# Attention projections: six products of a token block alternate between two weight halves, 128 bytes further apart

## The chip, the cores and the metric

The kernel runs on one core of a Trainium2 chip, in one launch. The metric is device time in microseconds of a whole run; the median of several runs counts. TensorE (PE in the profile, with its weight loads as PEld) multiplies, VectorE (DVE) and ScalarE (ACT) prepare operands and read results, GpSimd (POOL) helps, and SyncE (SP) issues nearly all loads.

## The reference, cut to what matters

Three transformer blocks run one after the other on 256 tokens of width 1024, all in float32. Each block does the following, with other attention rules in each:

```python
h = rms_norm(x, gain)
qkv = h @ w_qkv          # 1024 -> 9216 columns (first block), 3072 (second), 1536 + side columns (third)
x = x + attention(qkv) @ w_o
u = rms_norm(x, gain2) @ w_up
x = x + (silu(conv(u)[gate]) * conv(u)[val]) @ w_down
```

What concerns this change is `h @ w_qkv`.

## The kernel before, in words

**Split operands.** Every large product is made in three products of a rounded type: a float32 operand is split into a high part (rounded) and a low part (the rest), and hi·hi + hi·lo + lo·hi is summed in PSUM. The normalised tokens are held in `xg[:, k, x, :]`: `k` is one of 8 blocks of the 1024 inputs (`KT` = 8), `x` = 0 is the high part and `x` = 1 the low one, and the last index is the token. DVE makes the low part (L524) and counts `x_lo` up by one for every `k`.

**The weight stream.** All weights are read from memory in chunks of up to 1024 columns of 128 rows, in the order of use, into a ring of six buffers (`RING`). `load` in SyncE's program issues one chunk when `w_lo_done` says that the buffer six chunks ago has been split. ACT copies the chunk into `w_hi` (L418) and DVE writes `w_raw - w_hi` into `w_lo` (L426); TensorE waits for `w_lo_done`. The first three chunks are loaded and split in two halves (`half_split_hi`, `half_split_lo`, `load_half`).

**A projection chunk.** A "unit" is 384 result columns (`UNIT`; 392 for the first of the third block, `UNIT_F`) for all 256 tokens. It takes four chunks (`UCH`), and each chunk holds the weights of two blocks `k = 2q` and `k = 2q + 1`: two halves of 384 columns, one behind the other (`QCHUNK` = 768 columns). In `unit_chunk_pe` TensorE makes 12 products of a chunk: for each half `kk` and each block `t` of 128 tokens it makes three. The stationary operand is a 128×128 piece of `xg` and the moving operand is the weight half, 384 columns:

```python
nc.tensor.matmul(out, hi, wh, ...)   # L717
nc.tensor.matmul(out, hi, wl, ...)   # L718
nc.tensor.matmul(out, lo, wh, ...)   # L719
```

The two token blocks go to two banks of PSUM. A few chunks at the start of the first and second block (`EARLY`: the first four, and one) have an order of their own in `early_chunk_pe` (L643), and go on as parts of their operands become ready.

**Where the operands lie.** Buffers are laid one behind the other in the order in which they are named: six `w_raw` of 4096 bytes per partition, six `w_hi` of 4096, six `w_lo` of 4352 (a chunk and 64 spare columns), `x_all` of 8256, and `xg` of 16384. Within its buffer `w_lo` begins 16 or 32 columns in (`lo_at`: 64 or 128 bytes; 64 in all projections of attention). One column of a partition is 4 bytes, and a half is 1536 bytes.

**Other large products.** In the feed-forward stages the tokens move and the weights are stationary: the up projection makes a product of 512 columns (L458) and one of 256 (L460) for each `k`, the down projection three of 256 (L1897 to L1899). Six chunks ahead of the third block use three of 256 as well (L444 to L446).

**Order.** Each engine runs a program written out by hand, and PE's puts other work of attention (transposes, scores, sums with the values) between projection chunks. Nothing reorders it but the semaphores.

Of the kernel before, what the change touches and what calls it, by code (L numbers as in the profile page):

```python
# [49 lines left out]
LO_UP, LO_DOWN = 16, 32  # L50
CHUNK = KT * P
UNIT = 3 * P
QCHUNK = 2 * UNIT
UNIT_F = UNIT + HEADS_C
QCHUNK_F = 2 * UNIT_F
UCH = KT // 2


# [141 lines left out]
def build(nc, x_d, xa_d, stream_d, par_d, con_d, taps_d, out_d):  # L200
# [227 lines left out]


    def half_split_hi(eng, c, kk):  # L430
        part = slice(kk * UNIT, (kk + 1) * UNIT)
        eng.wait_ge(half_in[c] if kk == 0 else w_loaded[c], 16)
        nc.scalar.activation(w_hi[c][:, part], w_raw[c][:, part], ACT.Copy).then_inc(half_hi if kk == 0 else w_hi_done, 1)

    def half_split_lo(eng, c, kk):
        part = slice(kk * UNIT, (kk + 1) * UNIT)
        eng.wait_ge(half_hi if kk == 0 else w_hi_done, c + 1)
        nc.vector.tensor_tensor(w_lo(c)[:, part], w_raw[c][:, part], w_hi[c][:, part].bitcast(F32),
                                ALU.subtract).then_inc(half_lo if kk == 0 else w_lo_done, 1)
# [194 lines left out]
    def early_chunk_pe(eng, st, n):  # L634

        q, u = divmod(n, 2) if st == 0 else (n, 0)
        c = QKV_C0[st] + n
        s, k0 = c % RING, KT * 2 * st

        def term(x, part, kk, start=False, ends=False):  # L640
            k = 2 * q + kk
            for t in range(2):
                last = nc.tensor.matmul(bank(unit_bank(st, u, t), 0, UNIT), xg[:, k, x, t * P:(t + 1) * P],  # L643
                                        part[:, kk * UNIT:(kk + 1) * UNIT], start=start, stop=ends)
                if ends and t == 0:
                    last.then_inc(att[st].unit, 1)
            return last

        if st == 0 and n < HALVES:
            for kk in range(2):  # L650
                eng.wait_ge(half_hi if kk == 0 else w_hi_done, c + 1)
                eng.wait_ge(x_hi, 2 * q + kk + 1)
                term(0, w_hi[s], kk, start=(q == 0 and kk == 0))
                if u == 0:
                    eng.wait_ge(half_lo if kk == 0 else w_lo_done, c + 1)
                    term(0, w_lo(c), kk)
                eng.wait_ge(x_lo, 2 * q + kk + 1)
                last = term(1, w_hi[s], kk)
                if u == 1:
                    eng.wait_ge(half_lo if kk == 0 else w_lo_done, c + 1)  # L660
                    last = term(0, w_lo(c), kk)
        else:
            eng.wait_ge(w_hi_done, c + 1)
            eng.wait_ge(x_hi, k0 + 2 * q + 2)
            for kk in range(2):
                term(0, w_hi[s], kk)
            eng.wait_ge(x_lo, k0 + 2 * q + 2)
            for kk in range(2):
                term(1, w_hi[s], kk)
            eng.wait_ge(w_lo_done, c + 1)  # L670
            for kk in range(2):
                last = term(0, w_lo(c), kk, ends=(2 * q + kk == KT - 1))
        last.then_inc(tiles, 1)
# [9 lines left out]
    def unit_chunk_pe(eng, st, n):  # L683

        if (st, n) in EARLY:
            early_chunk_pe(eng, st, n)
            return
        a = att[st]
        u, q = divmod(n, UCH)
        if st == 0 and n < 2 * UCH:  # L690
            q, u = divmod(n, 2)
        c = QKV_C0[st] + n
        s = c % RING
        eng.wait_ge(w_lo_done, c + 1)
        if q == 0:
            if st == 0 and u > 2:
                if (u - 2) % 3 < 2:
                    eng.wait_ge(a.nm, 2 * (2 * ((u - 2) // 3) + (u - 2) % 3 + 1))
                    if (u - 2) % 3 == 0 and u - 2 >= joint_unit(0):
                        eng.wait_ge(a.olo, (u - 2) // 3 - 1)  # L700
                else:
                    v_wait(eng, 0, (u - 2) // 3)
            if st > 0 and u >= 2:
                eng.wait_ge(a.nm, 2 * (u - 1))
                eng.wait_ge(a.ve, 2 * (u - 1))
            if st == 2 and u < 2:
                eng.wait_ge(pre_out, (3, N_PRE)[u])
        width = UNIT_F if st == 2 and u == 0 else UNIT
        for kk in range(2):
            k = 2 * q + kk  # L710
            wh, wl = w_hi[s][:, kk * width:(kk + 1) * width], w_lo(c)[:, kk * width:(kk + 1) * width]
            if st < 2 and u == 0:
                eng.wait_ge(x_lo, KT * 2 * st + k + 1)
            for t in range(2):
                out = bank(unit_bank(st, u, t), 0, width)
                hi, lo = xg[:, k, 0, t * P:(t + 1) * P], xg[:, k, 1, t * P:(t + 1) * P]
                nc.tensor.matmul(out, hi, wh, start=(k == 0), stop=False)  # L717
                nc.tensor.matmul(out, hi, wl, start=False, stop=False)  # L718
                last = nc.tensor.matmul(out, lo, wh, start=False, stop=(k == KT - 1))  # L719
                if k == KT - 1 and t == 0:  # L720
                    last.then_inc(a.unit, 1)
        last.then_inc(tiles, 1)

    def unit_wait(eng, st, u, t):
# [1542 lines left out]
    with nc.Block() as block:  # L2267

        @block.sync
        def _(sp):  # L2270
            def load(c):
                s, w = c % RING, chunk_cols(c)
                sp.dma_start(w_raw[s][:, 0:w], stream_d[c, :, 0:w]).then_inc(w_loaded[s], 16)


            def load_half(c, kk):
                part = slice(kk * UNIT, (kk + 1) * UNIT)
                sp.dma_start(w_raw[c][:, part], stream_d[c, :, part]).then_inc(half_in[c] if kk == 0 else w_loaded[c], 16)

            def load_x(m, n, landed):  # L2280
                a, b = GAINS + m * TOK if m else 0, GAINS + (m + n) * TOK
                sp.dma_start(x_all[:, X0 - GAINS + a:X0 - GAINS + b], xa_d[:, a:b]).then_inc(landed, 16)

            load_x(0, 1, x_first)
            load_x(1, 1, x_in[0])
            for kk in range(2):
                load_half(1, kk)
            load_x(2, 2, x_in[1])
            for kk in range(2):
                load_half(2, kk)  # L2290
            load(3)
            load_x(4, 2, x_in[2])
            load(4)
            load(5)
            load_x(6, 2, x_in[3])
            sp.dma_start(con[:, 0:CON_MASKA], con_d[:, 0:CON_MASKA]).then_inc(con_in, 16)
            sp.dma_start(par[:, 0:PAR_FFN], par_d[:, 0:PAR_FFN]).then_inc(row_in, 16)
            for c in range(RING, N_CHUNKS):
                sp.wait_ge(w_lo_done, c - RING + 1)
                load(c)  # L2300
                if c == RING + 10:
                    sp.dma_start(con[:, CON_MASKA:], con_d[:, CON_MASKA:N_CON]).then_inc(rest_in, 16)
                if c == A_OUT:
                    sp.wait_ge(rest_in, 16)
                    sp.dma_start(par[:, PAR_FFN:], par_d[:, PAR_FFN:]).then_inc(rest_in, 16)
                if c == A_FFN:
                    sp.dma_start(mask_b, con_d[:, CON_MASK2:CON_MASK2 + 3 * P]).then_inc(taps_in, 16)
                if c == B_FFN + 2 * RING:
                    sp.wait_ge(att[1].mx, PAIRS_AB)
                    sp.wait_ge(taps_in, 16)  # L2310
                    sp.dma_start(taps[:], taps_d[:, :]).then_inc(taps_in, 16)
                if c == RING + 16:
                    sp.wait_ge(x_lo, KT)
                    sp.wait_ge(x_sq, KT)
                    for q in range(UCH):
                        sp.dma_start(xT[:, 2 * q:2 * q + 2], x_d[2 * q:2 * q + 2].rearrange("k p t -> p k t")).then_inc(x_in[q], 16)
            for m in range(0, KT, 2):
                sp.wait_ge(x_new, 5 * KT + m + 1)
                sp.dma_start(out_d[m], xT[:, m, :]).then_inc(stored, 16)
            sp.wait_ge(stored, 16 * KT)  # L2320
# [15 lines left out]
        @block.scalar  # L2336
        def _(act):
            for kk, landed in ((0, half_in[0]), (1, w_loaded[0])):
                part = slice(kk * UNIT, (kk + 1) * UNIT)
                act.dma_start(w_raw[0][:, part], stream_d[0, :, part]).then_inc(landed, 16)  # L2340
            nc.scalar.preload_act_table_set("natural_log_exp_and_others")
            half_split_hi(act, 0, 0)
# [89 lines left out]
def weight_stream(w):  # L2432
# [7 lines left out]
    def unit(cols):  # L2440

        width = sum(m.shape[1] for m in cols)
        for q in range(UCH):
            c = np.zeros((P, CHUNK), np.float32)
            for kk in range(2):
                k = 2 * q + kk
                c[:, kk * width:(kk + 1) * width] = np.concatenate([m[k * P:(k + 1) * P] for m in cols], axis=1)
            chunks.append(c)

    def outs(m, order):  # L2450
# [136 lines left out]
```

## Time and profile before

| what | value |
|---|---|
| median of 3 runs | 1027.61 us (1026.99 to 1027.81) |
| the profiled execution, its own time | 1026.79 us |
| its span, first to last instruction | 1024.9 us |
| PE busy | 1019.7 us (99%) |
| DVE, ACT, POOL busy | 879.9, 684.8, 350.3 us |
| granted TensorE clock | full, in all 40 slices |

The profiled execution lies 0.8 us under the median and has 1.9 us around its span. A product's recorded duration (about 340 ns for 384 columns) overlaps its neighbours, so the time that it costs is the distance from its start to the start of the next one. Starts are shown to 10 ns; over a run of many products the mean distance is known far better.

### The profile page before, as it was taken

To read this page: it belongs to the slowest core of one execution; us is meant where nothing else is said; L and a number is where in the kernel's file an instruction comes from. 1 tells how busy PE (TensorE), PEld (TensorE's weight loads), DVE (VectorE), ACT (ScalarE), POOL (GpSimd) and SP (SyncE) were. 2 spreads that over 40 slices of the span, in tenths; PEclk is the share of its full clock that TensorE was granted. 3 is DMA by queue.
4 is the path that set the end of the run, shared out by engine and by line. 5 is a ranking of instruction groups with operands and counts; after the bars stand their busy time and mean duration, and the time that the engine had idled before them with its cause. 6 is when DMAs were issued, how large, how long until landed. Compare 5 with 4: busy or idle time off the path is not lost.

```text
span 1024.9 us, 22177 instructions
## 1 busy us (share of the span) xinstructions
PE 1019.7 (99%) x8000; PEld 958.8 (94%) x8000; DVE 879.9 (86%) x1532; ACT 684.8 (67%) x1263; POOL 350.3 (34%) x370
## 2 busy tenths in 40 slices
PE   9999999999999999999999999999999999999998
PEld 8999999999999999999999899999998998999998
DVE  7987778787799998887887999988897879999886
ACT  7776676766766656577786766656696767565663
POOL 5312222121356533332111556333350025654332
PEclk9999999999999999999999999999999999999999
DMA  9754465554476656536454666666534536665651
GB/s 317 259 151 152 139 185 157 168 177 164 156 227 206 213 194 185 181 94 203 140 184 145 225 207 219 193 200 186 160 120 135 166 122 209 218 210 192 197 163 42
DMA packets 57896, 183.59 MB, mean 179 GB/s; under 512 B 6368, under 2 KB 9824, under 8 KB 57568
## 3 DMA queue, kind: packets, MB, share of 16 engines
q1 hardware_dynamic: 56960, 181.72, 55.7%
q8 instruction: 45, 0.74, 0.3%
q10 hardware_dynamic: 864, 0.92, 0.3%
q14 instruction: 27, 0.22, 0.1%
HBM read 181.56 MB, written 1.05 MB: 178 GB/s over the span
## 4 chain that ended last, share of the span: by engine, by line
PE 97%; DVE 2%; DMA 0%; ACT 0%; issue 0%; DVEq 0%
PE ps L458 22%; PE ps L460 11%; PE ps L717 10%; PE ps L719 10%; PE ps L718 9%; PE ps L1897 6%; PE ps L1898 6%; PE ps L1899 6%; PE ps L1363 2%; PE ps L1365 2%; PE ps L1364 2%; PE ps L643 1%; PE ps L915 1%; PE ps L810 1%; DVE w_lo L426 1%; PE ps L953 1%
## 5 line engine op out<-in xcount | busy, mean ns | idle before, releaser
L426 DVE TENSOR_TENSOR w_lo<-w_raw,w_hi 128x1024 fp32r<-128x1024 f32 (+2 forms) x369 | 440.4, 1211 | 31.4 <-ACT w_hi L418 30.8
L418 ACT ACTIVATE w_hi<-w_raw 128x1024 fp32r<-128x1024 f32 (+2 forms) x369 | 353.5, 972 | 116.4 <-PE ps L460 99.1
L458 PE MATMUL ps<-xg,w_hi 128*128 128x512 f32 x1056 | 363.1, 390 | 0.0
L460 PE MATMUL ps<-xg,w_lo 128*128 128x256 f32 x1056 | 291.5, 276 | 0.0
L458 PEld LDWEIGHTS ps<-xg,w_hi 128*128 128x128 f32 x1056 | 198.2, 188 | 40.1 <-DVE w_lo L426 0.8
L2022 POOL TENSOR_TENSOR prob_t<-prob_t,qkT 128x256 f32<-128x256 f32 x63 | 111.7, 1773 | 255.4 <-ACT prob_t L1943 255.4
L460 PEld LDWEIGHTS ps<-xg,w_lo 128*128 128x128 f32 x1056 | 198.2, 188 | 0.0
L717 PE MATMUL ps<-w_hi,xg 128*128 128x384 f32 (+1 forms) x556 | 192.3, 346 | 0.0
L719 PE MATMUL ps<-w_hi,xg 128*128 128x384 f32 (+1 forms) x556 | 187.3, 337 | 0.0
L718 PE MATMUL ps<-w_lo,xg 128*128 128x384 f32 (+1 forms) x556 | 185.7, 334 | 0.0
L1897 PE MATMUL ps<-g_hi,w_hi 128*128 128x256 f32 x528 | 146.1, 277 | 0.1
L1898 PE MATMUL ps<-g_lo,w_hi 128*128 128x256 f32 x528 | 145.8, 276 | 0.0
L1899 PE MATMUL ps<-g_hi,w_lo 128*128 128x256 f32 x528 | 145.8, 276 | 0.0
L2016 POOL TENSOR_TENSOR qkT<-prob,rms_r 128x256 f32<-128x256 f32 x132 | 123.7, 958 | 17.0 <-DVE prob L1957 12.0
L1990 DVE SCALAR_TENSOR_TENSOR qkT<-qkT,par 128x255 f32<-128x255 f32 (+1 forms) x264 | 112.3, 476 | 7.3 <-ACT qkT L1936 7.3
L1936 ACT ACTIVATE qkT<-qkT,par 128x256 f32<-128x256 f32 x132 | 78.0, 599 | 48.6 <-POOL qkT L2016 47.3
L717 PEld LDWEIGHTS ps<-w_hi,xg 128*128 128x128 f32 x556 | 104.2, 187 | 2.5 <-issue 1.5
L719 PEld LDWEIGHTS ps<-w_hi,xg 128*128 128x128 f32 x556 | 104.4, 188 | 0.0
L718 PEld LDWEIGHTS ps<-w_lo,xg 128*128 128x128 f32 x556 | 104.3, 188 | 0.1
L1897 PEld LDWEIGHTS ps<-g_hi,w_hi 128*128 128x128 f32 x528 | 99.1, 188 | 2.9 <-issue 0.4
L1898 PEld LDWEIGHTS ps<-g_lo,w_hi 128*128 128x128 f32 x528 | 99.1, 188 | 0.0
L1899 PEld LDWEIGHTS ps<-g_hi,w_lo 128*128 128x128 f32 x528 | 99.1, 188 | 0.0
(197 smaller groups left out, 1377.1 us busy)
## 6 DMA issues: line engine op xcount, KB each, us to landing
w_raw<-w_stream SPq DMA_DIRECT2D x228, 512.0 KB, 3.8
w_raw<-w_stream SPq DMA_DIRECT2D x137, 384.0 KB, 3.6
w_raw<-w_stream SPq DMA_DIRECT2D x4, 392.0 KB, 3.1
con<-consts SPq DMA_DIRECT2D x1, 1024.0 KB, 6.8
x_all<-x_t SPq DMA_DIRECT2D x4, 256.0 KB, 4.9
conv_taps<-taps SPq DMA_DIRECT2D x1, 1024.0 KB, 6.1
w_raw<-w_stream SPq DMA_DIRECT2D x4, 192.0 KB, 4.4
x_all<-x_a SPq DMA_DIRECT2D x3, 256.0 KB, 5.9
```

The source lines that it names most:

```text
L418: nc.scalar.activation(w_hi[s][:, 0:w], w_raw[s][:, 0:w], ACT.Copy).then_inc(w_hi_done, 1)
L426: nc.vector.tensor_tensor(w_lo(c)[:, 0:w], w_raw[s][:, 0:w], w_hi[s][:, 0:w].bitcast(F32), ALU.subtract).then_inc(w_lo_done, 1)
L458: nc.tensor.matmul(bank(b, 0, 2 * TOK), w_hi[s][:, k * P:(k + 1) * P], xg[:, k, :, :].rearrange("p h t -> p (h t)"), start=(k == 0), stop= ...
L460: last = nc.tensor.matmul(bank(b), w_lo(c)[:, k * P:(k + 1) * P], xg_hi[:, k, :], start=False, stop=(k == KT - 1), skip_group_check=True)
L717: nc.tensor.matmul(out, hi, wh, start=(k == 0), stop=False)
L718: nc.tensor.matmul(out, hi, wl, start=False, stop=False)
L719: last = nc.tensor.matmul(out, lo, wh, start=False, stop=(k == KT - 1))
L1897: nc.tensor.matmul(acc(m), wh, g_hi[b][:], start=first, stop=False, skip_group_check=True)
L1898: nc.tensor.matmul(acc(m), wh, g_lo[b][:], start=False, stop=False, skip_group_check=True)
L1899: last = nc.tensor.matmul(acc(m), wl, g_hi[b][:], start=False, stop=True, skip_group_check=True)
L1990: nc.vector.scalar_tensor_tensor(cv_s[b][s][:, k:TOK], up_s[b][s][:, 0:TOK - k], par_col(f, t, per, i, 4 * s + 2 - k), cv_s[b][s][:, k:TOK ...
L2016: nc.gpsimd.tensor_tensor(up_s[t % 2][s], up_sum[s], rms_r[:], ALU.mult).then_inc(F.up, 1)
```

## The change

The second half of a projection chunk no longer begins where the first ends but 32 columns (128 bytes) later: its offset `SECOND` is 416 columns instead of 384, for `w_raw`, `w_hi`, `w_lo` and in memory. A chunk so grows from 768 to 800 columns (from 784 to 808 for the unit with 392), all of which are loaded and split. And `unit_chunk_pe` makes its 12 products in another order: the token block is the outer loop, then the term (hi·wh, lo·wh, hi·wl), and the half is the inner loop. The count of products and their operands are the same. The wait for the tokens' low part, where there is one, asks for both blocks `k` before the first product of the chunk.

```diff
+SECOND = UNIT + 32
-QCHUNK = 2 * UNIT
+QCHUNK = SECOND + UNIT
-QCHUNK_F = 2 * UNIT_F
+QCHUNK_F = SECOND + UNIT_F
...
     def half_split_hi(eng, c, kk):
-        part = slice(kk * UNIT, (kk + 1) * UNIT)
+        part = slice(kk * SECOND, kk * SECOND + UNIT)
...
-                                        part[:, kk * UNIT:(kk + 1) * UNIT], start=start, stop=ends)
+                                        part[:, kk * SECOND:kk * SECOND + UNIT], start=start, stop=ends)
...
-        for kk in range(2):
-            k = 2 * q + kk
-            wh, wl = w_hi[s][:, kk * width:(kk + 1) * width], w_lo(c)[:, kk * width:(kk + 1) * width]
-            if st < 2 and u == 0:
-                eng.wait_ge(x_lo, KT * 2 * st + k + 1)
-            for t in range(2):
-                out = bank(unit_bank(st, u, t), 0, width)
-                hi, lo = xg[:, k, 0, t * P:(t + 1) * P], xg[:, k, 1, t * P:(t + 1) * P]
-                nc.tensor.matmul(out, hi, wh, start=(k == 0), stop=False)
-                nc.tensor.matmul(out, hi, wl, start=False, stop=False)
-                last = nc.tensor.matmul(out, lo, wh, start=False, stop=(k == KT - 1))
-                if k == KT - 1 and t == 0:
-                    last.then_inc(a.unit, 1)
+        w_part = [[part[:, kk * SECOND:kk * SECOND + width] for kk in range(2)] for part in (w_hi[s], w_lo(c))]
+        if st < 2 and u == 0:
+            eng.wait_ge(x_lo, KT * 2 * st + 2 * q + 2)
+        for t in range(2):
+            out = bank(unit_bank(st, u, t), 0, width)
+            for x, low in ((0, 0), (1, 0), (0, 1)):
+                for kk in range(2):
+                    k = 2 * q + kk
+                    last = nc.tensor.matmul(out, xg[:, k, x, t * P:(t + 1) * P], w_part[low][kk], start=(k == 0 and x + low == 0),
+                                            stop=(k == KT - 1 and low == 1))
+            if q == UCH - 1 and t == 0:
+                last.then_inc(a.unit, 1)
         last.then_inc(tiles, 1)
...
-                part = slice(kk * UNIT, (kk + 1) * UNIT)
+                part = slice(kk * SECOND, kk * SECOND + UNIT)
                 sp.dma_start(w_raw[c][:, part], stream_d[c, :, part]).then_inc(half_in[c] if kk == 0 else w_loaded[c], 16)
...
-                c[:, kk * width:(kk + 1) * width] = np.concatenate([m[k * P:(k + 1) * P] for m in cols], axis=1)
+                c[:, kk * SECOND:kk * SECOND + width] = np.concatenate([m[k * P:(k + 1) * P] for m in cols], axis=1)
```

## Rows read from the trace of the kernel before

**Rows 1.** The page: the chain that ended last, share of the span by engine.

```profile
PE 97%; DVE 2%; DMA 0%; ACT 0%; issue 0%; DVEq 0%
```

**Rows 2.** Waits of PE: who waited for what, us in total, times, longest.

```profile
PE ps L2327 <- DVE zero L2379: 1.1, 1, 1.1
PE ps L643 <- ACT w_hi L433: 0.4, 1, 0.4
PE ps L1363 <- DVE mix_lo L992: 0.3, 1, 0.3
```

**Rows 3.** Groups by shape on PE: busy us, mean ns of one, idle before.

```profile
L717 PE MATMUL ps<-w_hi,xg 128*128 128x384 f32 x540 | 186.7, 346 | 0.0
```

**Rows 4.** PE's timeline in a projection of the first block: start us, us, what.

```profile
23.27 0.33 PE L717 MATMUL ps<-w_hi,xg 128*128 128x384 f32 x1
23.44 0.33 PE L718 MATMUL ps<-w_lo,xg 128*128 128x384 f32 x1
23.61 0.34 PE L719 MATMUL ps<-w_hi,xg 128*128 128x384 f32 x1
23.79 0.33 PE L717 MATMUL ps<-w_hi,xg 128*128 128x384 f32 x1
...
30.55 0.33 PE L717 MATMUL ps<-w_hi,xg 128*128 128x384 f32 x1
```

**Rows 5.** PE's timeline in an up projection of a feed-forward stage.

```profile
300.05 0.39 PE L458 MATMUL ps<-xg,w_hi 128*128 128x512 f32 x1
...
302.77 0.39 PE L458 MATMUL ps<-xg,w_hi 128*128 128x512 f32 x1
```

**Rows 6.** PE's timeline in the six chunks ahead of the third block.

```profile
743.30 0.28 PE L444 MATMUL ps<-xg,w_hi 128*128 128x256 f32 x1
...
751.50 0.28 PE L444 MATMUL ps<-xg,w_hi 128*128 128x256 f32 x1
...
755.14 0.28 PE L444 MATMUL ps<-xg,w_hi 128*128 128x256 f32 x1
...
760.58 0.28 PE L444 MATMUL ps<-xg,w_hi 128*128 128x256 f32 x1
```

**Rows 7.** PE's timeline at other projection chunks of the second and third block.

```profile
457.94 1.56 PE L643 MATMUL ps<-w_hi,xg 128*128 128x384 f32 x8
459.34 0.86 PE L643 MATMUL ps<-w_lo,xg 128*128 128x384 f32 x4
...
474.60 0.34 PE L718 MATMUL ps<-w_lo,xg 128*128 128x384 f32 x1
...
478.44 0.34 PE L719 MATMUL ps<-w_hi,xg 128*128 128x384 f32 x1
...
760.92 0.34 PE L717 MATMUL ps<-w_hi,xg 128*128 128x392 f32 x1
...
764.86 0.34 PE L718 MATMUL ps<-w_lo,xg 128*128 128x392 f32 x1
```

**Rows 8.** DVE's and PE's timeline where the second block's projections begin.

```profile
451.59 0.48 DVE L524 SCALAR_TENSOR_TENSOR xg<-x_all,par,xg 128x256 fp32r<-128x256 f32 x1
...
451.69 0.34 PE L717 MATMUL ps<-w_hi,xg 128*128 128x384 f32 x1
...
453.26 0.63 DVE L524 SCALAR_TENSOR_TENSOR xg<-x_all,par,xg 128x256 fp32r<-128x256 f32 x1
```

**Rows 9.** Groups by shape on DVE: the splits of whole and of projection chunks.

```profile
L426 DVE TENSOR_TENSOR w_lo<-w_raw,w_hi 128x1024 fp32r<-128x1024 f32 x228 | 300.4, 1333 | 29.5 <-ACT w_hi L418 29.1
...
L426 DVE TENSOR_TENSOR w_lo<-w_raw,w_hi 128x768 fp32r<-128x768 f32 x137 | 136.0, 1014 | 1.8 <-ACT w_hi L418 1.6
```

**Rows 10.** Busy time of PE, PEld, DVE, ACT, POOL in the first block's projections; clock, DMA.

```profile
13.50:245.00 231.50, 231.39 (x2173) 227.32 (x2171) 183.54 (x351) 162.09 (x334) 62.62 (x81) 1.00 0.59 186
```

**Rows 11.** DVE's and PE's timeline at the fifth chunk, near the start.

```profile
12.30 1.93 DVE L426 TENSOR_TENSOR w_lo<-w_raw,w_hi 128x768 fp32r<-128x768 f32 x2
...
13.53 0.33 PE L717 MATMUL ps<-w_hi,xg 128*128 128x384 f32 x1
```

More of the change, by code:

```diff
@@ L2276, in load_half @@
             def load_half(c, kk):
-                part = slice(kk * UNIT, (kk + 1) * UNIT)
+                part = slice(kk * SECOND, kk * SECOND + UNIT)
                 sp.dma_start(w_raw[c][:, part], stream_d[c, :, part]).then_inc(half_in[c] if kk == 0 else w_loaded[c], 16)
@@ L2338, in _ @@
             for kk, landed in ((0, half_in[0]), (1, w_loaded[0])):
-                part = slice(kk * UNIT, (kk + 1) * UNIT)
+                part = slice(kk * SECOND, kk * SECOND + UNIT)
                 act.dma_start(w_raw[0][:, part], stream_d[0, :, part]).then_inc(landed, 16)
```

## The prediction

> **What bounds the kernel now.** I read the chain that ended last first: 97% of it is PE [rows 1]. Then PE's waits: three, 1.8 us together, none in a projection chunk [rows 2]. So PE has no hole to close, and a change inside the projections counts by what it does to the distance between one product's start and the next one's, almost one for one.
>
> The groups by shape give the count: 540 products of 384 columns on each of three lines [rows 3]. With the 48 of 392 columns (four chunks of 12) the changed function makes 1668, which is the 144 chunks of the three blocks, less five early ones, times 12. The mean duration in that group, 346 ns, is no price, since neighbours overlap. The timeline is. In a projection three products take 0.17, 0.17 and 0.18 us, and from 23.27 to 30.55 lie 42 distances: 7.28 / 42 = 173.3 ns each [rows 4].
>
> Is 173.3 ns what 384 columns must take? In an up projection 768 columns (512 + 256) take 2.72 us / 8 = 340.0 ns [rows 5], that is 0.4427 ns a column, and the same 113.3 ns for 256 columns stand in the settled part of the chunks ahead of the third block (5.44 us / 48) [rows 6]. By that rate 384 columns take 170.0 ns. A projection product so pays 3.3 ns more than the best rate of this trace. That is the whole room: 3.3 x 1620 = 5.4 us, and for the 392 columns (179.1 ns from 3.94 us / 22 [rows 7], against 173.5 by rate) 5.6 x 48 = 0.3 us. Together 5.7 us.
>
> What the 3.3 ns are, the trace does not say, but it gives three hints. First, the extra is not spread evenly: the longest of the three distances, 0.18 us, follows L719, after which the next product (L717) again reads `w_hi`, while after L717 and L718 the reading goes over to the other buffer [rows 4]. By the sizes in the code `w_hi` halves all begin at the same place modulo 256 bytes, and `w_lo` 64 bytes off it. Second, where each half is read twice in a row (the early chunk, L643), the distance is 1.40 us / 8 = 175.0 ns [rows 7]. Reading on at the same place modulo 256 so goes with the longer distances. Third, the same code with the same offsets modulo 256 runs at 8.20 us / 69 = 118.8 ns in three chunks and at 113.3 in the next three [rows 6]: the state in which the stream of products happens to run matters too, not the addresses alone.
>
> **The change part by part.** *The second half's place and the order.* The new order reads, in each token block, `w_hi` at 0, 128, 0, 128 and `w_lo` at 64, 192 (modulo 256, counted from `w_hi`). No product is followed by one that begins at the same place. The kind of step that costs 0.18 us is gone and all six are steps of 64 or 128. The trace has no step of 128, so I bound it: not under 170.0 (the best rate), and not over 175.4 (the 392-column products, whose second half is off by a distance that is no multiple of 256: 179.1 x 384 / 392 [rows 7]). For the value I take the two steps that do move, now: with the third between 175 and 180 ns, the other two share 520 less that, 170 to 172.5 each; the middle is 171.2 ns. That gains 2.1 x 1620 = 3.4 us. The 392-column products, if they come to the same rate (174.8), gain 4.3 x 48 = 0.2 us. Sum: 3.6 us; bounds: gain 5.7, loss 2.1 x 1668 = 3.5.
>
> On what moves an interval at all, the Trainium skill speaks against this change: "TensorE: Matmul & The Clock Gate", Step-by-step, says that TensorE reads the moving operand and the weights through two independent ports, so that loading the next weights takes nothing from the running product. By that rule no place of one operand against the other would cost anything and the sum would be zero gain. The 118.8 against 113.3 ns of one code [rows 6] shows that something beyond the column count does set the distance, though not which.
>
> *The wait for the low parts.* It exists only in the first unit of the first two blocks. In the second block, PE's first product stands at 451.69, right behind the stage before, and needs the low part of `k` = 0 alone; the low part of `k` = 1 ends at 451.59 + 0.48 = 452.07 [rows 8]. Before, the second half came 6 x 0.173 = 1.04 us later, which hid it. Now the chunk waits from 451.69 to about 452.1: 0.4 us, and the whole of PE's program is queued behind. The next chunk starts at 452.1 + 2.08 = 454.2; the low part of `k` = 3 is done at 453.26 + 0.63 = 453.89 [rows 8], so it does not wait. In the first block DVE makes the low parts ahead of the splits for which the same chunks wait anyway: nothing. Loss: 0.4 us.
>
> *32 more columns a chunk.* DVE's split costs (1333 - 1014) / 256 = 1.25 ns a column [rows 9], so 40 ns more for each of 137 whole chunks, 5.5 us in all; ACT and the loads grow by 4% as well. What hides it: in the first block's projections DVE is busy 183.5 of 231.5 us, ACT 162.1, DMA 59% [rows 10]; 93 splits x 40 ns take DVE to 187.2. The nearest point is the fifth chunk: two splits run from 12.30 to 14.23, so its own ends near 13.2 and PE starts at 13.53 [rows 11]. That lead of 0.3 us loses two splits' growth, 0.08 us. I count nothing; without any cover it would be the 5.5 us.
>
> *The earlier end of block 0.* In a unit's last chunk the first bank is complete after 6 products instead of 9, 0.52 us sooner. DVE and ACT may start reading sooner, but PE waits for none of them [rows 2]: nothing.
>
> *Sum.* -3.6 + 0.4 = -3.2 us: the profiled execution would go from 1026.79 to 1023.6. The median of the runs lies 0.8 us higher, so 1027.6 - 3.2 = 1024.4 us.
>
> **The rivals.** *No change.* The distance may depend on the moving read's start only modulo 128 (then 0 and 128 are one place), or on the state of the stream. For it: halves and ring buffers differ by multiples of 256 in every projection, so the trace never shows a step of 128. Against it: nothing direct. Then only the wait is left: 1027.6 + 0.4 = 1028.0 us. The skill's rule of two ports ends here too.
>
> *Slower: the streams no longer settle.* The settled run of 173.3 ns is one pattern of three products. Other patterns of the same lines are longer: 3.84 us / 22 = 174.5 ns in a run of the second block, 175.0 ns where each half comes twice in a row, 175.4 by the 392-column products [rows 7]; the unsettled 256-column products pay 5.5 ns over their rate [rows 6]. Six products with six different starts may have no settled pattern. At 175.0: 1.7 x 1668 + 0.4 = +3.2, 1030.8 us; at 175.4, 1031.5. It is slower by over the bound once the mean is above 174.3 ns. Against it: steps that move the start are the shorter ones in [rows 4].
>
> *DVE becomes the bound.* If the splits' growth came through in the chunks near the start or where attention's chain is tight, up to 5.5 us less the gain: 1027.6 - 3.2 + 5.5 = 1029.9. DVE's 21% of idle time [rows 10] speaks against it.
>
> **How the numbers follow.** About 0.2% (2.1 us) is what a measurement of this kernel can tell from no change. Faster by more needs a mean under 171.8 ns. Chances: the forecast's mechanism with a mean between 170 and 171.8, 0.47 (its own range 1022.0 to 1025.5); little or nothing, 0.28 (1025.5 to 1029.6); streams that do not settle, 0.22 (1029.7 to 1032, and above); DVE, 0.03. The range of 8 in 10 takes the first two and the nearer half of the third: 1022 to 1031.
>
> **What would show it.** In the timeline of a first-block projection six distances should sum to some 1.03 us instead of 1.04, with none of 0.18; a mean of 173 or more proves the forecast's main step wrong, whatever the total. The second block's first chunk should show a wait of PE of 0.4 us behind L524. DVE's split of 800 columns should take about 1.05 us with no wait of PE for it; such waits would make the covered term wrong. Another way to be wrong is a gain in the products that comes back as PE's waits for attention's own chain, which now has no wait to show its margin.

## The result and the profile after

The change makes the kernel slower: 1031.18 us (median of 6 runs, 1030.91 to 1031.7) against 1027.11 (1026.88 to 1027.81). The ratio is 1.0037, 95% interval 1.0028 to 1.0047, so +0.37%. The forecast was 1024.4 us with a range of 1022 to 1031; the median lies 0.2 us above the range, and on the other side of the kernel before. The profiled execution took 1031.7 us with a span of 1029.9.

The granted clock is full in all slices, as before. The chain that ended last, in the profile after, is as much PE's as before [rows 1], and PE's waits have one more line, the last:

```profile
PE 96%; DVE 2%; ACT 0%; DMA 0%; issue 0%; DVEq 0%; ACTq 0%
```

```profile
PE ps L2327 <- DVE zero L2379: 1.1, 1, 1.1
PE ps L1363 <- DVE mix_lo L992: 0.3, 1, 0.3
PE ps L644 <- ACT w_hi L434: 0.3, 1, 0.3
PE ps L718 <- DVE xg L525: 0.3, 1, 0.3
```

That wait is where the second block begins. In the timelines of DVE and PE there (the product's line is now L718, the low part's L525) the low part of `k` = 1 ends at 454.96 + 0.48 = 455.44, and the first product starts behind it, where it started at once before [rows 8]. In the last fence the first line is of the profile before, the others are of that after:

```profile
454.96 0.48 DVE L525 SCALAR_TENSOR_TENSOR xg<-x_all,par,xg 128x256 fp32r<-128x256 f32 x1
```

```profile
451.57 0.28 PE L1899 MATMUL ps<-g_hi,w_lo 128*128 128x256 f32 x1
...
455.01 0.28 PE L1899 MATMUL ps<-g_hi,w_lo 128*128 128x256 f32 x1
455.58 0.94 PE L718 MATMUL ps<-w_hi,xg 128*128 128x384 f32 x4 [0.29 <-DVE xg L525]
```

PE is idle for 0.29 us, but its next start comes later by more: from the last product of the stage before to the first of the projection it is 0.57 us, where before it was 451.69 - 451.57 = 0.12. So the wait costs 0.45 us.

The rest is in the products. In PE's timeline of a projection neighbours with one key are now one row; between the two `w_lo` rows lie 24 products:

```profile
71.94 0.51 PE L718 MATMUL ps<-w_lo,xg 128*128 128x384 f32 x2
72.29 0.86 PE L718 MATMUL ps<-w_hi,xg 128*128 128x384 f32 x4
72.98 0.52 PE L718 MATMUL ps<-w_lo,xg 128*128 128x384 f32 x2
...
76.17 0.51 PE L718 MATMUL ps<-w_lo,xg 128*128 128x384 f32 x2
```

4.23 us / 24 = 176.3 ns, where [rows 4] gave 173.3. For a mean over the kernel I take all 1487 distances between two neighbouring 384-column products that stand inside an unbroken run, without the first distance of a run and without the early chunks: 173.49 ns before, 175.74 after. So 2.25 ns x 1620 products of 384 columns = 3.6 us, and with the wait 4.1: about the 4.07 us between the medians. The 48 products of 392 columns did not change (183.7 and 183.4 ns in the mean of all their distances). (The two profiled spans differ by 4.9. In the profiled execution after, the early chunks also ended 0.75 us later, at 14.28 instead of 13.53. Single executions scatter there: the early code of before ends at 13.89 in e4's profile, that of after at 13.71 in e6's. Over all profiles the kernels with chunks of 800 columns or more end it at 13.71 to 14.28, the others at 13.48 to 13.94, so a part may come from the wider loads; the median of e8 below, which has them too, shows no cost.)

What the products do is still regular. The starts in the trace, which are in ns, give a run of distances that repeats: before, every three products (171, 173, 176); after, every 12 (a mean difference of 0.4 ns to the distance 12 products earlier, and of 3 ns or more to those one to six earlier). "Settled" below means that the distances of a run repeat like this. The stream after has settled too, in a longer pattern with distances of 170 to 181 ns.

The splits grew as said, in the groups by shape on DVE (before: [rows 9]), and no wait of PE names them:

```profile
L427 DVE TENSOR_TENSOR w_lo<-w_raw,w_hi 128x800 fp32r<-128x800 f32 x137 | 140.6, 1048 | 1.1 <-ACT w_hi L419 0.5
```

### The profile page after: what moved, and what is told of

It is laid out like the page before. It is cut to its first block, busy times and chain, and to the rows that moved or that the text cites. A ratio compares the mean times of both kernels' runs of the same rounds, so it can differ in the third digit from the quotient of the medians.

```text
span 1029.9 us, 22177 instructions
## 1 busy us (share of the span) xinstructions
PE 1024.5 (99%) x8000; PEld 962.9 (94%) x8000; DVE 884.6 (86%) x1532; ACT 688.1 (67%) x1263; POOL 352.2 (34%) x370
## 4 chain that ended last, share of the span: by engine, by line
PE 96%; DVE 2%; ACT 0%; DMA 0%; issue 0%; DVEq 0%; ACTq 0%
PE ps L718 29%; PE ps L459 22%; PE ps L461 11%; PE ps L1897 6%; PE ps L1899 5%; PE ps L1898 5%; PE ps L1363 2%; PE ps L1365 2%; PE ps L1364 2%; PE ps L644 1%; PE ps L915 1%; PE ps L810 1%; DVE w_lo L427 1%; PE ps L953 1%; PE ps L898 1%; PE ps L2152 1%
## 5 line engine op out<-in xcount | busy, mean ns | idle before, releaser
L427 DVE TENSOR_TENSOR w_lo<-w_raw,w_hi 128x1024 fp32r<-128x1024 f32 (+2 forms) x369 | 445.2, 1224 | 30.5 <-ACT w_hi L419 29.5
L718 PE MATMUL ps<-w_hi,xg 128*128 128x384 f32 (+1 forms) x1112 | 246.3, 343 | 0.3 <-DVE xg L525 0.3
L718 PEld LDWEIGHTS ps<-w_hi,xg 128*128 128x128 f32 x1112 | 194.6, 188 | 3.1 <-issue 2.0
L718 PE MATMUL ps<-w_lo,xg 128*128 128x384 f32 (+1 forms) x556 | 143.6, 339 | 0.0
L718 PEld LDWEIGHTS ps<-w_lo,xg 128*128 128x128 f32 x556 | 101.2, 188 | 0.0
L1957 DVE TENSOR_REDUCE prob<-ps 128x256 f32<-128x512 f32 x132 | 84.8, 681 | 3.8 <-PE ps L461 3.8
L1330 POOL TENSOR_TENSOR rot<-tokbuf,tab_a 128x192 f32<-128x192 f32 x16 | 19.8, 1239 | 166.0 <-DVE tokbuf L1199 166.0
```

Of the source, the lines that this page charges most:

```text
L427: nc.vector.tensor_tensor(w_lo(c)[:, 0:w], w_raw[s][:, 0:w], w_hi[s][:, 0:w].bitcast(F32), ALU.subtract).then_inc(w_lo_done, 1)
L718: last = nc.tensor.matmul(out, xg[:, k, x, t * P:(t + 1) * P], w_part[low][kk], start=(k == 0 and x + low == 0), stop=(k == KT - 1 and low ...
L1957: nc.vector.tensor_reduce(up_sum[s], bank(2 * b + s, 0, 2 * TOK).rearrange("p (h t) -> p t h", h=2), AXIS_X, ALU.add).then_inc(F.sum, 1)
```

## The experiments

Times are medians against the kernel before on the same chip. "Distance" is the mean over the 1487 products as above.

| kernel | distance, ns | time, us | before, us | ratio, 95% interval |
|---|---|---|---|---|
| before | 173.49 | | 1027.11 | |
| after | 175.74 | 1031.18 | 1027.11 | 1.0037 [1.0028, 1.0047] |
| e1 order only | 174.37 | 1029.50 | 1026.97 | 1.0024 [1.0015, 1.0033] |
| e2 distance only | 174.64 | 1028.80 | 1026.97 | 1.0017 [1.0008, 1.0026] |
| e6 late wait | 175.79 | 1030.88 | 1027.00 | 1.0036 [1.0022, 1.0050] |
| e7 settled places | 173.72 | 1027.31 | 1027.00 | 1.0003 [0.9994, 1.0012] |
| e8 wide chunks | 173.49 | 1027.20 | 1027.26 | 0.9999 [0.9990, 1.0008] |
| e9 order on settled places | 173.86 | 1028.05 | 1027.26 | 1.0007 [0.9998, 1.0016] |
| e10 second half 256 bytes on | 174.35 | 1029.53 | 1027.26 | 1.0019 [1.0010, 1.0028] |

**e1 and e2: the two parts alone.** The order of after with `SECOND = UNIT`, and the distance of after with the loops of before:

```diff
-SECOND = UNIT + 32
+SECOND = UNIT
...
```

```diff
...
-            wh, wl = w_hi[s][:, kk * width:(kk + 1) * width], w_lo(c)[:, kk * width:(kk + 1) * width]
+            wh, wl = w_hi[s][:, kk * SECOND:kk * SECOND + width], w_lo(c)[:, kk * SECOND:kk * SECOND + width]
```

> The new order of the six products and the joint wait for the low parts, with the halves where they were before. Theory O (the order costs: a half that is read twice in a row, or terms that no longer follow in threes, leave the settled pattern): projection products at some 175 to 176 ns, 3 to 4 us slower than before. Theory P (the place costs: the second half 128 bytes further is the bad part): products at 173.5 ns as before, and only the wait of 0.3 us where the second block begins, so 0.3 us slower.

> The second half 32 columns further, chunks of 800 columns, with the order and the waits of before. Theory P (the place costs): products at some 175 to 176 ns, 3 to 4 us slower than before. Theory O (the order costs): 173.5 ns and no change. Both together could also be needed; then each alone shows less than 1.5 us.

Each costs part of it: the order 0.9 ns a product and the wait, the distance of the second half 1.2 ns a product. PE's timeline with the distance alone shows 42 products in 77.50 - 70.16 = 7.34 us, 174.8 ns:

```profile
70.16 0.34 PE L719 MATMUL ps<-w_lo,xg 128*128 128x384 f32 x1
...
77.50 0.34 PE L719 MATMUL ps<-w_lo,xg 128*128 128x384 f32 x1
```

Neither theory alone holds; the parts nearly add up (0.9 + 1.2 against 2.25 together). Both streams settle: with the order alone every six products (169, 173, 173, 174, 176, 181 ns), with the distance alone every 24. The order's 2.5 us are 0.6 more than its products (1.4) and its wait (0.5 from start to start, 0.4 idle) explain, which its interval of 0.9 us either way covers.

**e3 and e5: many arrangements in one kernel.** In the first block every unit from the fourth on got places of its own (a place is where a read begins), in columns: the start of the first half, the distance of the second, the start of the low part.

```diff
+        return SWEEP[c // UCH]
...
+        w_part = [[part[:, first + kk * second:first + kk * second + width] for kk in range(2)] for part in (w_hi[s], w_lo(c))]
```

> One look at 21 arrangements in one kernel: in the first block each unit from the fourth on has its own start of the first half (0, 8, 16, 24, 32 or 48 columns in), distance of the second (384, 400, 416, 432 columns), start of the low part (0, 8, 16, 32, 48 columns) and order; results are the same sums. The distance between starts is read unit by unit. Theory S (the step between one moving read and the next counts, as in the forecast): the units whose low part lies as far in as the high one (no step) are the slowest, 175 ns or more, wherever the first half starts, and all steps of 64 or 128 bytes are near 171 to 173. Theory R (the moving read's place against that of the weights that are loaded meanwhile counts): moving all halves 64 bytes on changes the distance with all steps the same, and with the moving reads 64 bytes off the places of before, as in the feed-forward stages, some unit comes to 170 ns.

> A second look at 21 arrangements, unit by unit. Places are counted in bytes modulo 256 from the start of w_hi; the weights loaded meanwhile (xg) lie at 64. Theory R: a run settles at 173.3 ns where every moving read lies 0 to 64 bytes past that place, in either order: halves and low parts at 64 or 128 only (first half 16 columns in, second half 400 columns on; first half 32 in, low part 48 in) come to 173.3 to 173.7, and arrangements with a read at 0 or 192 alone stay at 175 to 177. Theory S (steps between reads): the two that alternate between 64 and 128 do better than those that do not step at all. In both cases units that repeat an arrangement of the first sweep (16, 0, 24 columns in without a low offset) give 173.3, 176.7 and 176.7 again.

The mean distance in a unit, without the first six of each run, from the starts in the trace (the rest of the 42 units lie between 173.3 and 176.7):

| order, first half, second half, low part | e3 | e5 |
|---|---|---|
| before, 0, 384, 16 (the kernel before) | 173.8 and 173.2 | 173.2 |
| before, 0, 384, 0 (no step between reads) | 176.7 | 174.0 |
| before, 16, 384, 0 (no step) | 173.3 | 173.6 |
| new, 16, 384, 0 | 173.4 | 173.3 |
| before, 24, 384, 0 (no step) | 176.7 | 173.3 |
| before, 12, 384, 0 (no step) | | 179.9 |
| new, 0, 384, 16 (e1's) | 174.1 | |
| before, 0, 416, 16 (e2's) | 174.5 | |
| new, 0, 416, 16 (the kernel after) | 176.5 | |
| new, 16, 416, 0 | 175.0 | |
| new, 16, 400, 0 (steps of 64 bytes) | | 176.6 |
| before, 16, 400, 0 (steps of 64 bytes) | | 173.6 |

Three readings. No unit is below 173.2 ns. Some units whose reads never change their place come to 173.3 as well as any: the step between reads (theory S, the forecast's) is not what makes products short. And places alone do not decide either (theory R): with the first half 24 columns in, 176.7 in one sweep and 173.3 in the other, in the same unit and the same buffers, so only what ran before it, or the execution, differs; with no offset at all, 176.7 in e3 and both in e5. There the unit runs one way first and the other later, with nothing changed but the buffers, which lie multiples of 256 bytes apart, and breaks for transposes. PE's timeline of that unit:

```profile
43.16 0.34 PE L733 MATMUL ps<-w_lo,xg 128*128 128x384 f32 x1
...
46.80 0.34 PE L733 MATMUL ps<-w_lo,xg 128*128 128x384 f32 x1
...
50.51 0.34 PE L733 MATMUL ps<-w_lo,xg 128*128 128x384 f32 x1
...
52.10 0.34 PE L733 MATMUL ps<-w_lo,xg 128*128 128x384 f32 x1
```

21 products in 3.64 us are 173.3 ns each; 9 products in 1.59 us are 176.7. The same code can settle in either of two patterns; how the run began is the likely reason, but no run sets it on purpose.

**e4: what a width costs by itself.** Behind the last stage of the kernel before, runs of 40 products of one width, with one stationary piece and moving reads of `xg`; nobody reads the result.

```diff
             ffn_stage(pe, 2, ffn_pe(2))
+            data = xg[:].rearrange("p k h t -> p (k h t)")
+            weights = data[:, 1024:1024 + P]
+            for n in range(40):
+                nc.tensor.matmul(bank(0, 0, 320), weights, data[:, 0:320], start=True, stop=True, skip_group_check=True)
```

> The kernel before, with 15 runs of 40 further products behind its last stage, which nobody reads: one stationary piece of xg, moving reads of xg of 256 to 512 columns, and of 384 columns from four starts. The time as a whole is some 100 us longer and says nothing. Theory G (the forecast's: 0.4427 ns a column): 384 columns 170.0 ns, 288 columns 127.5, 320 141.7, 448 198.3. Theory F (a fixed step of 6.7 ns for every 256 columns begun, beside the columns at full clock): 256 columns 113.3 ns and 512 columns 226.7 as in theory G, but 288 columns 133.3, 320 146.7, 384 173.3, 392 176.7, 448 200.0. By F the products of before had no room at all.

PE's timeline, one row for a run; the distance is the next row's start less this one's, over 40:

```profile
1022.11 7.10 PE L2338 MATMUL ps<-xg 128*128 128x384 f32 x40
1029.05 4.95 PE L2340 MATMUL ps<-xg 128*128 128x256 f32 x40
1033.84 5.43 PE L2342 MATMUL ps<-xg 128*128 128x288 f32 x40
1039.11 6.03 PE L2344 MATMUL ps<-xg 128*128 128x320 f32 x40
1044.97 6.56 PE L2346 MATMUL ps<-xg 128*128 128x352 f32 x40
1051.38 7.09 PE L2348 MATMUL ps<-xg 128*128 128x376 f32 x40
1058.31 7.25 PE L2350 MATMUL ps<-xg 128*128 128x392 f32 x40
1065.40 7.38 PE L2352 MATMUL ps<-xg 128*128 128x400 f32 x40
1072.61 7.69 PE L2354 MATMUL ps<-xg 128*128 128x416 f32 x40
1080.14 8.28 PE L2356 MATMUL ps<-xg 128*128 128x448 f32 x40
1088.26 8.83 PE L2358 MATMUL ps<-xg 128*128 128x480 f32 x40
1096.93 9.25 PE L2360 MATMUL ps<-xg 128*128 128x512 f32 x40
1106.02 7.10 PE L2362 MATMUL ps<-xg 128*128 128x384 f32 x40
1112.95 7.19 PE L2364 MATMUL ps<-xg 128*128 128x384 f32 x40
1119.98 7.23 PE L2366 MATMUL ps<-xg 128*128 128x384 f32 x40
```

320 columns take 146.5 ns, 352 take 160.3, 384 take 173.5, 400 take 180.3 and 512 take 227.3. That is theory F (146.7, 160.0, 173.3, 180.0, 226.7): the columns at 2.4 GHz and about 13.3 ns. Theory G's 141.7 for 320 columns and 170.0 for 384 do not occur. F does not hold at all widths: 288 columns take 131.8 (F 133.3, G 127.5), and others lie above it: 376 at 173.3 (F 170.0), 392 at 177.3 (176.7), 416 at 188.3 (186.7), 448 at 203.0 (200.0) and 480 at 216.8 (213.3). And 256 take 119.8, where the feed-forward stages and the settled chunks have 113.3 [rows 5, 6]: a run of identical products does not always show the best rate of its width. So e4 alone does not prove that 384 columns cannot go under 173.3 ns; it is e3 and e5, where 42 units did not, that make it likely.

The start matters too: 384 columns read from 16 columns in take 173.3 (1106.02 to 1112.95), from 32 columns in 175.8 (1112.95 to 1119.98) and, from the starts in the trace, from 48 in 176.7. In bytes modulo 256 from the start of `w_hi`, where `xg` by the sizes of the buffers lies at 64, the four starts of e4 are 64, 128, 192 and 0. The units of e3 without a step read at the same four places and give nearly the same: 173.3, 173.4, 175.9 and 176.7 ns. So a place costs something by itself, though e5's unit at place 0, with both values, shows that it is not alone. The kernel after adds reads at 128 and 192; whether the one at 192 is what costs, no run separates.

**e6: the wait taken away.** The kernel after, with the wait for a low part ahead of the products that read it:

```diff
-            eng.wait_ge(x_lo, KT * 2 * st + 2 * q + 2)
+            eng.wait_ge(x_hi, KT * 2 * st + 2 * q + 2)
...
+                    if st < 2 and u == 0 and t == 0 and x == 1:
+                        eng.wait_ge(x_lo, KT * 2 * st + k + 1)
```

> The kernel after, where a chunk of the first unit waits for both high parts first and for each low part only ahead of the products that read it. Expected by every theory: the wait of 0.3 us where the second block begins is gone and the products stay at 175.8 ns, so 0.3 us less than after, still some 3.7 us slower than before. If the wait cost more than it shows, for instance through what follows it, the gain would be 1 us or more.

PE's waits no longer name L525, the products stay at 175.79 ns, and the time is 3.9 us above its kernel before, where after is 4.07 above: 0.2 us less, which the intervals don't separate from the 0.45 us of the wait or from nothing. The wait is a small term.

**e7 and e9: places that settle.** All halves 16 columns in, the low part not offset, no bytes between the halves (96 for the 392 columns); e7 with the order of before, e9 with that of after.

```diff
+FIRST = 16
...
-            return LO_DOWN if f == 2 and c < C_QKV else LO_UP
+            return LO_DOWN if f == 2 and c < C_QKV else 0
...
+            f0 = FIRST + kk * (width if width == UNIT else SECOND_F)
+            wh, wl = w_hi[s][:, f0:f0 + width], w_lo(c)[:, f0:f0 + width]
```

> The order of before in all projections, with both halves 16 columns further in and the low part not offset, so that all moving reads begin at one place, 64 bytes past the high part's of before; chunks of 784 columns (816 with the 392-column unit). Theory S (steps between reads are what makes products short): no read steps at all, so 175 ns or more and 2 to 4 us slower than before. Theory R with floor F: 173.3 to 173.5 ns, no shorter than before's settled products, and the same time as before within 0.2%. Theory G: 170 to 171 ns and 4 us faster.

> The order and the joint wait of after, on the arrangement in which every moving read begins at one place, 64 bytes further in, and nothing is 128 bytes apart. Theory U (the order costs only where it keeps the products from settling): products at 173.4 ns, and no more than the wait of 0.3 us slower than before. Theory O (the order itself costs, by its six same-bank products in a row or its pairs of one term): 174 ns or more and 1 to 2.5 us slower, as with the order alone.

In both kernels the products settle at 173.3 to 173.5 ns in every unit behind the early chunks, but for the 392 columns and, in e7, one unit (174.2). In e9's timeline 42 products lie between these two rows, 7.28 us, the 173.3 ns of [rows 4] in the order of after:

```profile
69.70 0.51 PE L720 MATMUL ps<-w_lo,xg 128*128 128x384 f32 x2
...
76.98 0.51 PE L720 MATMUL ps<-w_lo,xg 128*128 128x384 f32 x2
```

So the new order is not dear in itself, nor are its six products in a row into one bank. e9's time is 0.8 us above before; 0.4 us of it is the wait (its idle time), and its interval covers the rest. And in e7, with the halves settled at this place, the kernel is no faster than before.

**e8: the bytes alone.** Chunks of 800 columns, the halves where they were.

```diff
-QCHUNK = 2 * UNIT
+QCHUNK = 2 * UNIT + 32
```

> The kernel before, with chunks of 800 columns (808 for the wider unit) loaded and split as after, the 32 more at the end and never read. If the splits' growth is covered, as the prediction has it: the same time as before, products at 173.5 ns, no wait of PE for a split. If it is not: up to 5.5 us slower, and waits of PE for w_lo.

DVE's group and PE's waits in e8:

```profile
L426 DVE TENSOR_TENSOR w_lo<-w_raw,w_hi 128x800 fp32r<-128x800 f32 x137 | 140.4, 1046 | 0.9 <-ACT w_hi L418 0.5
```

```profile
PE ps L2327 <- DVE zero L2379: 1.1, 1, 1.1
PE ps L1363 <- DVE mix_lo L992: 0.3, 1, 0.3
PE ps L643 <- ACT w_hi L433: 0.3, 1, 0.3
```

No wait for a split is added (the last line, for `w_hi`, stands in [rows 2] too) and the time is that of before: the growth is covered.

**e10: 256 bytes instead of 128.**

```diff
-SECOND = UNIT + 32
+SECOND = UNIT + 64
```

> The kernel after with the second half 64 columns (256 bytes) further instead of 32. If places count modulo 256 bytes, as the forecast took them: like the order alone, products at 174.0 ns and some 2.5 us slower than before. If any move of the second half costs, or the bytes that are loaded and split for nothing: 175.8 ns or more, 4 us slower or more.

The distance is that of the order alone (174.35 against 174.37, and 173.6 to 174.5 in all units of 384 columns behind the early ones), though twice as many bytes are loaded for nothing. Product by product, 94% of the distances in the two traces agree within 1 ns; between e1 and after 34% do. For the second half, a place is the same place 256 bytes on; 128 is another one.

## Why the prediction was wrong

**The step that failed first** is "By that rate 384 columns take 170.0 ns", and with it the room worked out from it, "Together 5.7 us". The rate of 0.4427 ns a column was taken from 256 and 512 columns and carried to a width between them. Measured, 384 columns settle at 173.3 ns at best (e4, and no unit of the 42 in e3 and e5 is below 173.2). The settled run of [rows 4] already had that: the room of 5.7 us was taken from a rate that no run here reached at this width, and most products had nothing left to gain that any run found.

**The second** is the value 171.2 ns, read from two of three distances. Within a settled pattern the three distances share out one sum; that one of them is longer says nothing of what the others would be without it. In e7 and e9, where no read steps, they are 173, 173 and 174 ns in place of 171, 173 and 176: the same 520. So the steps of the reading were the wrong cause.

**What happened in its place** is the rival "the streams no longer settle", with a chance of 0.22: the products came to 175.7 ns where it had 175.0 to 175.4, and the time to 1031.2 where it had 1030.8 to 1031.5. Its size was right, and of its mechanism a half: other patterns of the same products are longer. That six products "may have no settled pattern" did not happen; they settled in a longer one, of 12 products. (Nor are their starts six different ones: by the prediction's own list they are four, 0, 128, 64 and 192.) The third hint, that one code runs at two distances [rows 6], was in the rows and should have given this rival more weight: a change of order or place can move a settled stream into a longer pattern.

**The smaller terms held.** The wait: 0.4 us foreseen, 0.45 measured from start to start (0.29 of it idle). The splits: 40 ns more foreseen, 34 measured (1048 - 1014), covered (e8). The places modulo 256 bytes: shown for the second half (e10). The 392 columns: 0.2 us of gain foreseen, none measured. The earlier end of block 0 brought nothing that the waits show.

**The rule of two read ports.** What the Trainium skill says there ("TensorE: Matmul & The Clock Gate", Step-by-step: two independent read ports) was set beside the case of no change. In e4 the same product with the same weights takes 173.3 or 175.8 ns by the start of its moving read, so places do cost here. Whether the loading of the weights is the other party, the runs do not show.

**Open** is what gives a pattern its length, and why the places and the order of after lead to a longer one. The experiments show that each part does so alone, that the two nearly add up, and that the order costs the products nothing where all reads begin at the place of e7; they do not show the mechanism.

## What to carry to other kernels

Before pricing a gain from a better rate, measure that rate at the very shape: a cost per column fitted to two widths need not hold between them. A run of identical products gives a first value, and several starts and orders a better one, since the 256 columns of e4 took 119.8 ns where the kernel has 113.3. Where a tuned stream of products already repeats the shortest pattern that any run shows, changes of order and of operand places are more likely to cost than to gain: of those tried here some cost nothing and none gained. Look in the trace for stretches of the same code at two distances, since they tell that the pattern can be lost.

## What the runs showed that I had not expected

Products of 320, 352, 384, 400 and 512 columns, settled, cost their columns at 2.4 GHz plus some 13.3 ns (e4), those of 256 in the feed-forward stages plus 6.7 [rows 5, 6] and in e4 plus 13, those of 376, 448 and 480 in e4 plus 16 to 17, so 384 columns are dearer by the column (0.451 ns) than 256 or 512 (0.443). And one arrangement can run steadily at 173.3 or at 176.7 ns (e3 and e5).
